# Two layer transitions in a decoder trunk on one core: the plain residual is transposed and the root's reciprocal applied afterwards

## The reference

```
def _rmsnorm(x, gain):
    xf = x.astype(jnp.float32)
    y = xf * lax.rsqrt(jnp.mean(xf * xf, axis=-1, keepdims=True) + NORM_EPS)
    return (y * gain.astype(jnp.float32)).astype(x.dtype)
def _swiglu(h, w_gate, w_up, w_down):
    return (jax.nn.silu(h @ w_gate) * (h @ w_up)) @ w_down
def _s5(h, w_in, ...):
    u = (h @ w_in).astype(f32)      # then B u, a scan over tokens, C x
    ...                             # y + d_skip * u, gelu, @ w_out, gate
h = h + retention(_rmsnorm(h, norm_mix[0]), ...)
h = h + _swiglu(_rmsnorm(h, norm_ffn[0]), ...)
h = h + _s5(_rmsnorm(h, norm_mix[1]), ...)
h = h + _moe(_rmsnorm(h, norm_ffn[1]), ...)
return _rmsnorm(h, norm_final)
```

## Time and profile before

| | us |
|---|---|
| median of 3 runs | 1607.85 (1606.59 to 1608.47) |
| profiled execution, its own time | 1607.26 |
| span of its trace (first to last instruction) | 1605.5 |
| PE matmul busy | 1575.9 (98%) |
| DVE busy | 1197.3 (75%) |
| ACT busy | 985.9 (61%) |
| POOL busy | 265.4 (17%) |
| mean granted clock of TensorE | 0.996 |

### The profile page before, as it was taken

How to read it: one execution, slowest core, us unless ns; L and a number is a source line. 1 busy time by engine, 2 the same in 40 slices (tenths; PEclk the granted TensorE clock), 3 DMA queues, 4 the chain that set the end, 5 groups by cost and what they waited for, 6 DMA issues and landing times.

```text
span 1605.5 us, 23474 instructions
## 1 busy us (share of the span) xinstructions
PE 1575.9 (98%) x9434; PEld 1316.4 (82%) x9434; DVE 1197.3 (75%) x783; ACT 985.9 (61%) x733; POOL 265.4 (17%) x245
## 2 busy tenths in 40 slices
PE   8999999999999999999999999999999999999998
PEld 7888889999988778788888888888888888888886
DVE  5556565544456746888888888888888888888897
ACT  5443444333444346777777777777777777777775
POOL 5599315300035205200000000000000000000200
PEclk9999999999999999999999999999999999999999
DMA  9544637855511185999999999999999999999994
GB/s 342 166 157 156 209 122 269 299 203 184 184 53 55 43 315 192 392 381 346 386 369 362 390 373 356 386 370 352 380 377 359 387 367 354 388 371 348 398 393 155
DMA packets 202142, 469.17 MB, mean 292 GB/s; under 512 B 7784, under 2 KB 20288, under 8 KB 202064
## 3 DMA queue, kind: packets, MB, share of 16 engines
q1 hardware_dynamic: 199872, 461.13, 79.4%
q0 software_dynamic: 2048, 6.88, 1.4%
q10 hardware_dynamic: 144, 0.07, 0.0%
HBM read 461.23 MB, written 15.21 MB: 297 GB/s over the span
## 4 chain that ended last, share of the span: by engine, by line
PE 94%; DVE 3%; ACT 1%; issue 1%; DMA 0%; SPq 0%; DVEq 0%; ACTq 0%
PE PS L1672 91%; PE PS L1765 2%; DVE weights_lo L1247 1%; DMA weights_raw<-in_ret_w_in 0%; ACT c_padded L865 0%; DVE residual L1247 0%; PE PS L2092 0%; DVE x_transposed_lo L1274 0%; ACT weights_hi L865 0%; PE PS L1952 0%; DVE scan L1247 0%; DVE states L1247 0%; DVE scan_tmp L1247 0%; ACT magnitude_table L865 0%; PE PS L2056 0%
## 5 line engine op out<-in xcount | busy, mean ns | idle before, releaser
L1247 DVE TENSOR_TENSOR weights_lo<-weights_raw,weights_hi 128x2048 fp32r<-128x2048 f32 (+1 forms) x419 | 966.5, 2316 | 299.0 <-ACT weights_hi L865 297.3
L865 ACT ACTIVATE weights_hi<-weights_raw 128x2048 fp32r<-128x2048 f32 (+1 forms) x419 | 800.8, 1912 | 344.0 <-PE PS L1672 333.1
L1672 PE MATMUL PS<-weights_hi,gathered_hi 128*128 128x512 f32 x896 | 355.2, 396 | 0.3 <-DVE gathered_lo L1553 0.3
L1672 PE MATMUL PS<-weights_hi,gathered_lo 128*128 128x512 f32 x896 | 355.1, 396 | 0.0
L1672 PE MATMUL PS<-weights_lo,gathered_hi 128*128 128x512 f32 x896 | 352.2, 393 | 0.0
L1672 PE MATMUL PS<-weights_hi,act_transposed_hi 128*128 128x512 f32 x624 | 253.0, 406 | 1.6 <-DVE weights_lo L1247 1.1
L1672 PE MATMUL PS<-weights_hi,act_transposed_lo 128*128 128x512 f32 x624 | 247.0, 396 | 0.0
L1672 PE MATMUL PS<-weights_lo,act_transposed_hi 128*128 128x512 f32 x624 | 245.8, 394 | 0.0
L1672 PEld LDWEIGHTS PS<-weights_lo,gathered_hi 128*128 128x128 f32 x896 | 168.2, 188 | 41.3
L1672 PEld LDWEIGHTS PS<-weights_hi,gathered_lo 128*128 128x128 f32 x896 | 168.2, 188 | 41.3
L1672 PEld LDWEIGHTS PS<-weights_hi,gathered_hi 128*128 128x128 f32 x896 | 168.2, 188 | 39.8 <-DVE gathered_lo L1553 0.4
(11 more groups left out here) (266 smaller groups left out, 1265.6 us busy)
## 6 DMA issues: line engine op xcount, KB each, us to landing
weights_raw<-in_moe_w_up SPq DMA_DIRECT2D x111, 1024.0 KB, 6.8
weights_raw<-in_moe_w_down SPq DMA_DIRECT2D x111, 1024.0 KB, 6.6
weights_raw<-in_moe_w_gate SPq DMA_DIRECT2D x110, 1024.0 KB, 6.8
weights_raw<-in_ret_w_in SPq DMA_DIRECT2D x24, 1024.0 KB, 6.2
weights_raw<-in_ffn_w_gate SPq DMA_DIRECT2D x14, 1024.0 KB, 5.1
weights_raw<-in_ffn_w_up SPq DMA_DIRECT2D x14, 1024.0 KB, 5.1
weights_raw<-in_ffn_w_down SPq DMA_DIRECT2D x14, 1024.0 KB, 4.9
weights_raw<-in_ret_w_out SPq DMA_DIRECT2D x8, 1024.0 KB, 5.0
```

What stands on the lines that cost most here:

```text
L865: return nc.scalar.activation(o, i, ACT.Copy)
L1247: return nc.vector.tensor_tensor(o, a, b, op)
L1672: return nc.tensor.matmul(o, l, r, start=start, stop=stop)
```

## The change

- **Sums in pieces.** The last output unit of retention and of dense (`closing_unit`) runs through its four results one after the other instead of all in one sweep, and says when results 0 and 1 (`part_done`), 2 (`part_done`) and 3 (`used`) are complete. DVE adds the first 128x1024 and then two halves of 128x512 as they come. The number of matmuls is the same.
- **The plain residual is turned.** `plain(i)` turns the residual itself, tokens 0 to 127 after the first sum, the rest after the last. hn is no longer written scaled. Sums of squares, both now on ACT, lie before and behind ACT's `norm_split`; root and reciprocal follow.
- **The reciprocal comes later.** DVE writes two diagonal matrices (128x128), PE multiplies them with ones (`rstd_to_columns`, two full-precision matmuls) so that every partition holds all 256 reciprocals, DVE copies them out (`take_row`). In dense, DVE scales the gate on its way out of PSUM (two of 128x512), ACT's Silu reads that, and a further 128x1024 multiplication scales the product; PE waits for `gate_scaled` and `up_read` where it waited for `silu_done` and `mult_done`. In S5, DVE's `scale_u` takes the place of ACT's `copy_u`; for quarter 1 it stands inside `states_of(0)`, for 2 and 3 behind `states_of(q - 1)`.
- **Direct terms in bank 3.** They use columns 256 to 447 of bank 3 and no longer wait for u; `turn_b(q, 1)` follows them; `s5_in` waits for `direct_ready`. ACT's order changes with it, in quarters 2 and 3 as the diff shows it for quarter 1.
- **idle_work.** 7 + 5 + 5 calls around transition 1 become one of 16 behind the transposes; 7 + 5 around transition 2 go.
- POOL's load of C also waits for the root of transition 1 (`std_done`).

```diff
+        rstd_row = small("rstd_of_columns", [SEQ])
+        rstd_diag = [place(f"rstd_diagonal{i}", [TT, P], F32, offset) for i, offset in enumerate((W_OFF + 24576, 12288))]
...
             pool.wait_ge(used, FFN_U0 + 1)
+            pool.wait_ge(std_done, 2)
...
+            def norm_later(i):
+
+                load_sqrt()
+                act.wait_ge(sum0_ready, i)
+                nc.scalar.activation(hn[:, 0, :], resid[:, 0, :], ACT.Square, accum_out=ssq[:, 0:1]).then_inc(ssq0_done, 1)
+                norm_split(i)
+                act.wait_ge(resid_ready, i)
+                nc.scalar.activation(hn[:, 1, :], resid[:, 1, :], ACT.Square, accum_out=ssq[:, 1:2]).then_inc(ssq1_done, 1)
                 act.wait_ge(ssq0_done, i + 1)
                 act.wait_ge(ssq1_done, i + 1)
-                if i == 0:
-                    act.wait_ge(x_landed[1], 16)
                 nc.scalar.activation(std[:, :], ssq[:, :], ACT.Sqrt, scale=1.0 / D, bias=eps).then_inc(std_done, 1)
...
-                        if i == f0 + 4:
-                            act.wait_ge(used, FFN_U0 + f0 + 2)
-                            if s:
-                                act.wait_ge(mult_done, s)
-                            nc.scalar.activation(gated[:, :, :], PS[:, 0:TT, :], ACT.Silu).then_inc(silu_done, 1)
...
+                        if i == f0 + 5:
+                            act.wait_ge(gate_scaled, s + 1)
+                            nc.scalar.activation(gated[:, :, :], gated[:, :, :], ACT.Silu).then_inc(silu_done, 1)
...
-                rows = PS[:, 4, 0:QKT * (STEP - 1) * 32].rearrange("p (k n) -> p k n", n=32)
+                rows = PS[:, 3, TERMS:TERMS + QKT * (STEP - 1) * 32].rearrange("p (k n) -> p k n", n=32)
...
             split_hi(S5_U0 + 3)
             copy_b(1, 0)
             pad_c(1)
+            copy_direct(1)
+            copy_b(1, 1)
             magnitudes(1)
-            copy_u(1)
-            copy_b(1, 1)
-            copy_direct(1)
             split_hi(S5_U0 + 4)
...
+            def norm_later(i, n):
+
+                dve.wait_ge(part_done, 2 * i - 1)
+                tt(resid[:, 0, :], resid[:, 0, :], PS[:, 4:6, :].rearrange("p a b -> p (a b)"), ALU.add).then_inc(sum0_ready, 1)
+                dve.wait_ge(part_done, 2 * i)
+                tt(resid[:, 1, 0:512], resid[:, 1, 0:512], PS[:, 6, :], ALU.add)
+                dve.wait_ge(used, n)
+                tt(resid[:, 1, 512:D], resid[:, 1, 512:D], PS[:, 7, :], ALU.add).then_inc(resid_ready, 1)
+                norm_split(i)
                 dve.wait_ge(std_done, i + 1)
                 nc.vector.reciprocal(rstd[:, :], std[:, :]).then_inc(rstd_done, 1)
                 dve.wait_ge(rstd_done, i + 1)
-                nc.vector.tensor_scalar(hn[:, 0, :], resid[:, 0, :], rstd[:, 0:1], None, ALU.mult).then_inc(hn0_ready, 1)
+                for t in range(TT):
+                    ins = nc.vector.tensor_scalar(rstd_diag[i - 1][:, t, :], ident, rstd[:, t:t + 1], None, ALU.mult)
+                ins.then_inc(diag_ready, 1)
+
+            def take_row(i, bank):
+
+                dve.wait_ge(row_done, i)
+                link(nc.vector.tensor_copy(rstd_row[:, :], PS[:, bank, 0:SEQ]))
+
+            def by_token(rows, n):
+                return rows.rearrange("p (n t) -> p n t", n=n), rstd_row[:, :].unsqueeze(1).to_broadcast([P, n, SEQ])
...
+                        if i == f0 + 4:
+                            dve.wait_ge(used, FFN_U0 + f0 + 2)
+                            if s:
+                                dve.wait_ge(up_read, s)
+                            for t in range(TT):
+                                gate, row = by_token(PS[:, t, :], 2)
+                                ins = tt(gated[:, t, :].rearrange("p (n t) -> p n t", n=2), gate, row, ALU.mult)
+                            ins.then_inc(gate_scaled, 1)
                         if i == f0 + 6:
                             dve.wait_ge(silu_done, s + 1)
                             dve.wait_ge(used, FFN_U0 + f0 + 4)
                             if s:
                                 dve.wait_ge(act_hi, s)
                                 dve.wait_ge(act_lo, s)
-                            tt(act_rows[:, :, :], gated[:, :, :], PS[:, TT:2 * TT, :], ALU.mult).then_inc(mult_done, 1)
+                            tt(act_rows[:, :, :], gated[:, :, :], PS[:, TT:2 * TT, :], ALU.mult).then_inc(up_read, 1)
+                            dve.wait_ge(up_read, s + 1)
+                            rows, row = by_token(act_rows[:, :, :].rearrange("p t f -> p (t f)"), FT)
+                            tt(rows, rows, row, ALU.mult).then_inc(mult_done, 1)
...
-            dve.wait_ge(used, FFN_U0)
-            add_out()
-            norm_rows(1)
-            norm_split(1)
+            norm_later(1, FFN_U0)
             split_lo(FFN_U0 + 2)
+            take_row(1, 7)
             dense()
...
-            dve.wait_ge(used, S5_U0)
-            add_out()
-            dve.wait_ge(c_ready, 1)
-            norm_rows(2)
-            norm_split(2)
-            split_lo(S5_U0 + 2)
+            norm_later(2, S5_U0)
+            take_row(2, 1)
...
+                if within:
+                    within()
...
-            states_of(0)
+            def scale_u(c):
+
+                dve.wait_ge(used, S5_U0 + c + 1)
+                u, row = by_token(PS[:, U_BANK[c], :], 2)
+                tt(u_t[:, 2 * c:2 * c + 2, :], u, row, ALU.mult).then_inc(u_copied, 1)
+
+            scale_u(0)
+            split_lo(S5_U0 + 2)
+            states_of(0, lambda: scale_u(1))
             split_lo(S5_U0 + 3)
             states_of(1)
+            scale_u(2)
             add_y(0)
             split_lo(S5_U0 + 4)
             states_of(2)
+            scale_u(3)
             add_y(1)
...
+            def closing_unit(n, a_hi, a_lo):
+
+                split_ready(n)
+                hi = w_hi[:, n % SPLIT, :].rearrange("p (k n) -> p k n", k=2)
+                lo = w_lo[:, n % SPLIT, :].rearrange("p (k n) -> p k n", k=2)
+                for t, dh, done in ((0, 0, None), (0, 1, part_done), (1, 0, part_done), (1, 1, used)):
+                    c = slice(dh * 512, dh * 512 + 512)
+                    for k in range(2):
+                        ins = product3(PS[:, out_bank(t, dh), :], a_hi[:, t, 2 + k, :], a_lo[:, t, 2 + k, :],
+                                       hi[:, k, c], lo[:, k, c], False, k == 1)
+                    if done:
+                        ins.then_inc(done, 1)
...
+            def plain(i):
+
+                for t, (ready, n) in enumerate(((sum0_ready, i), (resid_ready, i))):
+                    pe.wait_ge(ready, n)
+                    for kt in range(KT):
+                        c = kt % 2 * SEQ + t * P
+                        ins = nc.tensor.transpose(PS[:, kt // 2, c:c + P], resid[:, t, kt * P:(kt + 1) * P], ident)
+                        if t and kt % 2:
+                            ins.then_inc(xt_done, 1)
+
+            def rstd_to_columns(i, bank):
+
+                pe.wait_ge(diag_ready, i)
+                for t in range(TT):
+                    ins = mm(PS[:, bank, t * P:(t + 1) * P], ones, rstd_diag[i - 1][:, t, :], True, True)
+                ins.then_inc(row_done, 1)
...
-                        pe.wait_ge(silu_done, s)
+                        pe.wait_ge(gate_scaled, s)
                     for half in range(2):
                         f_cols_unit(n + half, half, 0, 1 if s == 0 else None)
+                        if s == 0 and half == 0:
+                            rstd_to_columns(1, 7)
                     if s:
-                        pe.wait_ge(mult_done, s)
+                        pe.wait_ge(up_read, s)
                     for half in range(2):
                         f_cols_unit(n + 2 + half, half, TT)
                     if s == 0:
+                        pe.wait_ge(gate_scaled, 1)
...
-                for half in range(2):
-                    down(STEPS - 1, half, FFN_U0 + FFN_UNITS - 2 + half)
+                down(STEPS - 1, 0, FFN_U0 + FFN_UNITS - 2)
+                closing_unit(FFN_U0 + FFN_UNITS - 1, ht_hi[(STEPS - 1) % 2], ht_lo[(STEPS - 1) % 2])
...
-            norm_wait(1, 0)
-            norm(1)
+            head_out(HEADS - 1, 0, RET_UNITS - 2)
+            closing_unit(RET_UNITS - 1, ht_hi[0], ht_lo[0])
+
+
+            plain(1)
+            idle_work(16, 4)
...
-            idle_work(7, 0)
-            pe.wait_ge(resid_ready, 2)
+            plain(2)
             pe.wait_ge(setup_done, 1)
             turn_b(0, 0, 6)
             turn_b(0, 1, 4)
-            pe.wait_ge(std_done, 3)
-            idle_work(5, 0)
-            norm(2)
...
+                if q:
+                    pe.wait_ge(bu_read, q)
...
+                pe.wait_ge(direct_ready, q + 1)
                 for a in range(QKT):
+                    pe.wait_ge(bt_copied, 2 * q + a + 1)
...
-            cols_unit(S5_U0, 0, 2)
+            cols_unit(S5_U0, 0, 2, between=lambda: rstd_to_columns(2, 1))
```

(8 more changed lines are left out.)

107 lines of the change are left out of this document (44 added, 63 removed).

## The result

| | before | after |
|---|---|---|
| median of 7 runs each, in the same comparison | 1606.76 us | 1599.82 us |
| lowest and highest | 1603.72 to 1608.47 | 1595.93 to 1602.08 |
| ratio, 95% interval | | 0.9948 (0.9936 to 0.9960) |
| a later comparison on one chip (11 and 6 runs) | 1606.26 us | 1599.56 us, ratio 0.9957 (0.9943 to 0.9971) |

The ratios are 8.4 us (6.4 to 10.3) and 6.9 us (4.7 to 9.2) less on 1607.85. The forecast was 6.1 less. The direction held and the gain was 0.8 to 2.3 us larger than forecast.

What follows compares the result with a forecast made beforehand. Matmuls on PE bound the kernel, so only PE's waits and idle work can be won. Terms -2.6 - 3.0 - 0.9 + 0.4 = -6.1 gave 1601.7 us from the median 1607.85; own range 1599.8 to 1603.3, wider 1598.6 to 1605.2.

Steps and rivals of the forecast that it cites:

- the chain of ACT at transition 2: ACT's work up to direct's copy, ending 13.7 us after dense's last product and setting `s5_in(0)`, before at 16.7; gain 3.0.
- Transition 1: Retention to dense: dense starts 5.9 us after the last product, behind idle work, where it took 9.0; net -2.6.
- row of reciprocals: Two full-precision matmuls added after dense's first unit, four instructions, 0.5 us.
- Dense: DVE's added 2.6 us per step hide in 33.6 us of PE: cost 0, bounds 0 and +1.2 per step.
- Transition 2: Dense to S5: input unit starts 4.6 us earlier, `s5_in(0)` waits for direct's copy; gain 3.0, bounds 1.5 to 4.6.
- Rival A: Transition 2: transposes do not hold the clock, a 6.5 us low stretch over the first S5 unit; 1603.4, chance 0.14.
- Quarters: S5's quarters 1 to 3: shorter chain to the direct terms with the eight transposes behind them; 0.3 us per quarter, -0.9.
- The last chain: End of `s5_in(3)` to `s5_out(3)`, 11.9 us: it stays, but DVE is free 0.4 late, +0.4.
- Rival C: S5 swallows its part: POOL's addition ends behind its reader, 0.6 to 1.1 us per quarter; 1605.0, chance 0.12.
- The clock: Low stretches at 489.9 to 496.4 and 527.6 to 530.6 cost 4.75 us in all and stay as long.

Runs made afterwards that it cites:

- e1: Changed kernel with 4 idle calls in place of 16 behind the first transition's transposes; ratio 0.9919 to the kernel before, 1596.58 us.
- e7: Changed kernel with one more 128x1024 multiplication on DVE in every step of dense, its result unread; ratio 0.9941 to the kernel before, 1596.73 us.
- e2: Changed kernel with ACT's copy of quarter 0's direct terms ahead of the rounding of the third S5 unit; ratio 0.9938 to the kernel before, 1599.22 us.
- e3: Changed kernel with the sums in one piece again, DVE waiting for the whole last unit; ratio 0.9953 to the kernel before, 1602.12 us.
- e11: Changed kernel with no idle work at all at the first transition; ratio 0.9941 to the kernel before, 1597.62 us.
- e8: Changed kernel with the old order of PE and ACT inside quarters 1 to 3; ratio 0.9949 to the kernel before, 1598.25 us.
- e9: Changed kernel with 4 idle calls in PE's stop of 1.1 us ahead of `s5_in(0)`; ratio 0.9933 to the kernel before, 1598.23 us.
- before again: The kernel before with no edit, run once more for a second trace; one run, 1609.45 us.
- e5: On top of e2, POOL's padding of B for the next quarter begins with the last power; ratio 0.9947 to the kernel before, 1596.33 us.
- e6: Changed kernel with the edits of e1, e2 and e5 together; ratio 0.9933 to the kernel before, 1594.17 us.
- e10: On top of e6, DVE's split of the fourth S5 unit waits for POOL's addition of quarter 0; ratio 0.9907 to the kernel before, 1592.90 us.

## Why the prediction was wrong in size and right in its main mechanisms

**Which step failed.** Of the stages' -8.3 against -6.1, 0.55 is scatter behind the S5. The largest real miss is one term of the sum, the chain of ACT at transition 2: forecast T + 13.7 and a gain of 3.0, measured T + 12.8 and 3.85. Transition 1 adds 0.3, and the S5's rows, whose sum is near the forecast by luck, 0.4.

**Transition 1: right, 0.4 too small.** Dense starts behind the idle work, as said, at T + 5.5 instead of T + 5.9: the idle work begins at T + 2.0 instead of T + 2.15, and dense's first matmul starts 3.5 behind its begin instead of 3.7, beside the last calls. With the row of reciprocals (0.61 for four instructions, forecast 0.5) -2.9 against -2.6. e1 shows that idle work was the bound and that x was there 1.1 earlier, at T + 4.4 (forecast 4.55).

**Dense: right.** PE waited nowhere; +0.56 is the row of reciprocals. e7 shows that the cover is deeper than what the change uses.

**Transition 2: the mis-sized term.** I forecast -3.0 and it is -3.85. The mechanism (the S5 unit at T + 4.5, a stop of PE that ends with ACT's copy of direct) is there; the stop is 1.1 instead of 2. The step that failed is "ACT: ... so T + 6.5; ... then direct 0.31: T + 13.7". I added seven durations of ACT end to end. In the rows above most of ACT's instructions start 0.1 to 0.2 before the shown end of the one ahead of them, and the first tile came 0.2 earlier, so the chain ends at T + 12.7. e2 shows that with the rounding moved the unit's end is the bound, 0.6 further down.

**Rival A fell.** The clock stays at 1.00 from 466 to 481 with 32 transposes alone for 4.4 us, and so it does in all twelve traces with this transition (in e3 behind a stop of 1.3 more). The Trainium skill, TensorE: Matmul & The Clock Gate, Part 4 on transposes, says that a transpose does not count as busy time of PE in the same way. By that they should not have held it; these traces do not bear it out. e11 has as long a gap between last product and first unit (T + 4.4), with 16 transposes and then a stop of 2.2 us, and there it fell. In those 4.4 us PE's work differs in the second half alone; with one trace of e11 that is an observation, not a rule.

**Quarters: one quarter right, the reason wrong, the sum right by luck.** 17.96 per quarter against 18.25 at full clock (before, from the unit at 532.76 to that at 551.01) is the forecast -0.3. The direct terms start 3.3 behind the end of the first turn of B, where I had 3.1. e8 shows that the gain does not come from the order; that leaves u's copy. The last chain took 12.2 for 12.0, +0.2 where I had +0.4.

The row to `s5_out(3)` is -0.70 for a forecast of -0.5, but it holds terms that I did not have. Low clock cost this kernel 3.0 there (15.97 against e9's 12.94) and before again 2.1 (its `s5_out(0)` and `s5_out(2)`, 6.24 and 5.87 for 5.0 each). PE's breaks for nothing that the profile shows (last section) made `s5_in` 0.8, 0.7 and 0.7 longer in quarters 0, 2 and 3 of before again than in e9, while e9 loses 0.9 in `s5_out(0)`. And e9 waits for POOL, 0.63. With no low clock e9 takes 66.96 for the row and 46.08 for the next. Less the 2.1, before again would take 67.4, and it took 47.13. So at full clock the two rows are worth 1.5 (an estimate from these numbers) where the table has 0.9, and part of it is breaks that went and not work that was saved.

**Rival C was half there all the time.** POOL's addition did not swallow the gain, but I read 1.6 us of slack ahead of its reader from a trace in which the unit before it ran at half clock. At full clock that slack is a wait: 0.60 in the second trace of before, 0.54 in e3, 0.80 in e5, 0.97 in e6. e10 takes it away. The forecast left 0 for it, and gave the full wait to rival C alone. By the Trainium skill, SBUF — State Buffer, "SBUF: two separate sides", the pair of ports that the two engines share is held for whole instructions; 3.36 beside the split against 1.29 without it agrees.

**The clock.** I let the low stretches cost what they did, and for the pair of traces in the table the S5's two rows differ in it by 1.8 us (3.0 + 0.9 here, 2.1 in before again). Yet two traces of one kernel differ by 4.0 us in the routing part (15.27 and 19.30). Against its first trace the change looked 5.2 better (1607.26 to 1602.08), by the medians 6.9 to 8.4, by the stages of the pair 7.7 without the last row. The forecast stood on one execution, and its own range, 3.5 us wide, had no room for that. What starts or spares the low stretch of the routing part stays open; no run was made on it.

## What to carry to other kernels

A slack is read at the clock it will have: a reader that ran at half clock hides a producer that is late at full clock, so look at a second trace before you cost an edit at nothing. When a chain of short instructions on one engine sets the end, take starts to starts from the trace and not the sum of durations. Idle work that guards the clock is sized by removing it step by step: here 16 calls cost 1.1 us, 4 cost nothing, and 0, in the one trace of it, gave the gain back.

## What the runs showed of the hardware

- After the last product, the granted clock stayed at 1.00 over 4.4 us with transposes alone (eleven traces, and e3, where a stop of 1.3 stands ahead of them); over 2.2 us of them followed by a stop of 2.2 it did not (one trace, e11: 0.50 for 3.4 us, from 0.6 behind the stop).
- POOL's 128x512 addition took 3.36 us beside DVE's 128x2048 subtraction and 1.29 without it. Its 128x256 padding took 2.93 when it began just after that subtraction (e2), 1.65 when it began 0.9 ahead of its end (after), and 0.92 without it (both).
- PE stands still for 0.2 to 1.2 us at a time in S5's small matmuls for nothing that the profile shows. The place goes largely with the program: in `s5_in(2)` both traces of before break after 69 of 128 matmuls, and the changed kernel's don't. The length changes from trace to trace (in `s5_out(0)` the changed kernel has 0.58 in one trace and none above 0.15 in the other). With fewer idle calls at transition 1 (e1, e6, e10, e11) such breaks stand in `s5_out(2)`, 1.19 and 0.43 in e10, where the others have none above 0.2. Two instructions of the second trace of before:

```profile
519.75 2.32 PE L1672 MATMUL PS<-u_transposed,b_transposed 32*128 32x64 f32 x69
522.25 2.09 PE L1672 MATMUL PS<-u_transposed,b_transposed 32*128 32x64 f32 x59 [0.19 <-issue]
```

The second group stands still for 0.19 before it, and the whole of `s5_in(2)` takes 4.52 where the changed kernel's takes 3.86. I have not found the cause.
